# Front of a hybrid decoder step rewritten: token squares on two engines, first unit tile beside the gate tile, first head ahead of the branch product, recurrent turns at fixed tiles, padded rows

## The chip, the core and the metric

The kernel runs on one core of a Trainium2 chip. The core has five engines with their own instruction queues, which run each queue in order: TensorE (PE, with its weight loads as PEld), VectorE (DVE), ScalarE (ACT), GpSimd (POOL) and SyncE (SP), which here only issues DMAs. They meet at semaphores. TensorE writes to PSUM; the other data lies in SBUF. The metric is the device time of one execution in microseconds; 1193.46 us is the median of three runs of the kernel before (1191.86 to 1193.92).

## What is computed

One step of a hybrid decoder layer over 592 tokens: 16 meta tokens and 512 prompt tokens in one sequence, and 8 samples of 8 tokens with their own states. Width is 1024. Cut to what matters here:

```python
xn = rms_norm(x, norm1_g)
z  = xn @ w_in + b_in         # u | q | k | v | o | i-gate | f-gate | merge gate A | merge gate B
uc = causal_dwconv(u, lru_conv_buf, lru_conv_w, lru_conv_b)        # width 4
r, i = sigmoid(blockdiag(uc, w_r) + b_r), sigmoid(blockdiag(uc, w_i) + b_i)
a  = exp(-8 * r * softplus(-lambda))
h_t = a_t * h_{t-1} + sqrt(1 - a_t**2) * (i_t * uc_t)              # RG-LRU, scan over positions
hb = mlstm(q, k, v, i-gate, log_sigmoid(f-gate))                   # 4 heads, chunks, running max
merged = sigmoid(gA) * (h @ w_branch_a) + sigmoid(gB) * (hb @ w_branch_b)
x = x + merged @ w_out
x = x + ConvFFN(rms_norm(x, norm2_g))
```

Each prompt row starts from zero states, each sample from the states given; all new states are outputs.

## The kernel before

Everything is held with features on the 128 partitions and the 592 tokens along the row (T; two halves of 296 for PSUM). Products are made in split precision: a weight tile of 1024 x 128 arrives in `stage` (two slots) by a DMA on SP's queue (`load`, L429), ScalarE copies its high part to `whi` (`hi`, L744), GpSimd subtracts it to get the low part `wlo` (`lo`, L715), and TensorE multiplies high by high, high by low and low by high in 48 matmuls (`split_product`, L1675; `gemm`, L1686). Weight tiles and PSUM tiles are each numbered; `begin` (L1670) waits until the PSUM tile two places earlier is evicted, and `hi` for a weight tile waits until the tile two places earlier, which used the same slot, is finished. These numbers are constants (`B_U`, `T_U` and so on), and each engine's list is written out by hand in its own block.

The front of the layer, up to the first mLSTM score, runs in this order on TensorE: transposes of the token rows, with the tile of the two small gates (`gate_step`) between them; transposes of parameter rows; eight unit tiles (u); eight merge-gate tiles (A); eight branch tiles (h @ w_branch_a); eight tiles of the first head (k, v, q, o) with token-major copies of k and v; transposes of the gate rows. Before it, ScalarE squares the five token tiles one after the other and takes roots (L769), and VectorE scales by the reciprocals (L1122).

The recurrence works on one feature tile at a time, a turn: VectorE's convolution over prompt and samples apart (`conv`), TensorE's four gate matmuls into `bank`, ScalarE's two sigmoids, tanh and exponential, VectorE's products, ScalarE's root, VectorE's scan over time, ScalarE's high part and VectorE's low part of h. The unit and merge-gate tiles run in loops of pairs with one turn in each pair (`with_lru`, `u_pair`, `ga_pair`). One pair of buffers `ri` and `th` serves all turns. The gate weights of a turn (`lru_load`) are loaded by four DMAs between two weight tiles, after TensorE has finished the turn before:

```python
sp.wait_ge(w_lo, b - 1)
load(b, (b0 + j) % 2, w_in, ds(c0 + 256 * i + 128 * j, P))
if j == 0:
    sp.wait_ge(lru_ps, p)
    lru_load(p)
```

VectorE's chain for the mLSTM gates (`log1p_exp`, running maximum, running sum, `gate_rows`) stands behind the eight branch evictions. Its result goes through a DRAM buffer to SBUF (`spread_load`) for the head loop.

## Time and profile before

| | before |
|---|---|
| median of three runs | 1193.46 us |
| the profiled execution, its own time | 1192.03 us |
| its span, first to last instruction | 1190.1 us |
| mean granted clock of TensorE | 0.989 |
| TensorE busy | 1136.5 us |
| start of the first unit tile | 34.43 us |
| start of the first mLSTM score | 290.41 us |

TensorE is busy nearly all the time, so the profile is read by its idle and slowed stretches: what a wait of TensorE is put down to, and which engine's queue that engine's instruction stood in. "Busy" of an overlapped engine (VectorE's instructions that stand still behind GpSimd count as busy) says little alone.

### The profile page before, as it was taken

The numbers are of one execution on the slowest core, as the hardware profiler recorded it, in microseconds if no ns is written. First come the engines' busy times: TensorE is split into PE (matmuls) and PEld (weight loads), VectorE is DVE, ScalarE is ACT, GpSimd is POOL, SyncE is SP. The second block draws the span as 40 slices with busy tenths as digits, with TensorE's granted clock in tenths as the row PEclk, the third lists the DMA queues.
The fourth block names the chain that finished last, engine by engine and source line by source line (L and its number), as shares of the span: only waits on it lengthen the run. The fifth ranks groups of instructions, "written<-read, shape, count | busy, mean of one in ns | idle before, by whom it ended". The sixth has DMA issues, their size and how long they took to land.

```text
span 1190.1 us, 20521 instructions
## 1 busy us (share of the span) xinstructions
PE 1136.5 (95%) x8286; PEld 1106.4 (93%) x8286; DVE 652.3 (55%) x1056; ACT 403.4 (34%) x503; POOL 357.6 (30%) x163
## 2 busy tenths in 40 slices
PE   4997998999999999999998999999999999999996
PEld 4896998999999999989988999999999999999996
DVE  3689553273226328146264333999991069999302
ACT  5566891135323322323132333322221122222213
POOL 3132223433221313122212334433334334343420
PEclk9998999999999999999998999999999999999998
DMA  6122222226136235244244233322323222323312
GB/s 161 39 75 54 60 73 71 76 75 184 53 86 202 59 111 172 54 124 134 54 133 135 73 89 90 89 80 82 102 84 98 69 75 71 89 72 101 88 35 84
DMA packets 181030, 108.76 MB, mean 91 GB/s; under 512 B 8981, under 2 KB 177381, under 8 KB 180952
## 3 DMA queue, kind: packets, MB, share of 16 engines
q1 hardware_dynamic: 180952, 107.63, 31.4%
q8 instruction: 60, 0.98, 0.3%
q14 instruction: 18, 0.15, 0.0%
HBM read 95.19 MB, written 12.41 MB: 90 GB/s over the span
## 4 chain that ended last, share of the span: by engine, by line
PE 83%; issue 11%; DVE 3%; POOL 2%; ACT 1%; POOLq 0%; ACTq 0%; DVEq 0%
PE ring L1682 36%; PE ring L2072 21%; PE bank L2072 16%; POOL wlo L718 2%; PE bank L1895 2%; PE bank L1880 1%; PE bank L1944 1%; PE ring L1787 1%; PE bank L1864 1%; PE bank L1849 1%; PE bank L1922 1%; PE bank L1884 1%; PE bank L1872 1%; DVE y L1119 1%; DVE n_tmp L1446 0%
## 5 line engine op out<-in xcount | busy, mean ns | idle before, releaser
L718 POOL TENSOR_TENSOR wlo<-stage,whi 128x1024 fp32r<-128x1024 f32 x80 | 195.1, 2440 | 527.1 <-ACT whi L749 527.1
L1682 PE MATMUL ring<-xh,whi 128*128 128x296 f32 x1024 | 233.3, 309 | 15.6 <-POOL wlo L718 12.5
L1682 PE MATMUL ring<-xh,wlo 128*128 128x296 f32 x1024 | 224.7, 301 | 0.0
L1682 PE MATMUL ring<-xl,whi 128*128 128x296 f32 x1024 | 224.7, 301 | 0.0
L1682 PEld LDWEIGHTS ring<-xh,whi 128*128 128x128 f32 x1024 | 167.4, 191 | 28.2 <-issue 20.2
L1682 PEld LDWEIGHTS ring<-xl,whi 128*128 128x128 f32 x1024 | 168.5, 191 | 0.0
L1682 PEld LDWEIGHTS ring<-xh,wlo 128*128 128x128 f32 x1024 | 167.9, 190 | 0.0
L736 POOL TENSOR_TENSOR wlo<-stage,whi 128x1024 fp32r<-128x1024 f32 (+1 forms) x40 | 105.8, 2647 | 176.1 <-ACT whi L1032 176.1
L749 ACT ACTIVATE whi<-stage 128x1024 fp32r<-128x1024 f32 x81 | 85.2, 1052 | 47.9 <-PE ring L1682 35.7
L1032 ACT ACTIVATE whi<-stage 128x1024 fp32r<-128x1024 f32 (+1 forms) x40 | 45.9, 1151 | 94.4 <-PE ring L2072 59.2
L736 POOL TENSOR_TENSOR wlo_third<-stage,whi_third 128x1024 fp32r<-128x1024 f32 (+1 forms) x20 | 51.4, 2572 | 87.1 <-ACT whi_third L1032 87.1
L1119 DVE SCALAR_TENSOR_TENSOR conv<-up,cols,conv 128x608 f32<-128x608 f32 x88 | 74.9, 852 | 3.1
L2072 PE MATMUL ring<-xh,whi 128*128 128x296 f32 x256 | 56.0, 300 | 0.0
L1065 ACT ACTIVATE conv<-conv 128x608 f32<-128x608 f32 x22 | 15.7, 713 | 118.3 <-DVE conv L1119 118.3
L2072 PE MATMUL ring<-xh,wlo 128*128 128x296 f32 x256 | 55.7, 299 | 0.0
L2072 PE MATMUL ring<-xl,whi 128*128 128x296 f32 x256 | 55.6, 299 | 0.0
L1657 DVE TENSOR_TENSOR resid<-ring,resid 128x592 f32<-128x592 f32 x10 | 7.7, 774 | 86.6 <-PE ring L2072 86.6
L1433 DVE COPY hb<-bank 128x256 f32<-128x256 f32 (+1 forms) x20 | 8.0, 402 | 83.9 <-PE bank L1884 74.5
L1631 DVE TENSOR_TENSOR product<-conv 128x528 f32<-128x528 f32 x22 | 53.0, 2411 | 0.0
L1603 DVE COPY up<-cols 128x16 f32<-128x16 f32 x44 | 45.4, 1031 | 0.0
L2072 PE MATMUL bank<-xh,whi 128*128 128x296 f32 x192 | 42.0, 300 | 0.0
L2072 PE MATMUL bank<-xh,wlo 128*128 128x296 f32 x192 | 41.7, 299 | 0.0
(337 smaller groups left out, 2389.5 us busy)
## 6 DMA issues: line engine op xcount, KB each, us to landing
stage<-in_w_in SPq DMA_DIRECT2D x56, 512.0 KB, 3.8
stage<-in_w_up SPq DMA_DIRECT2D x44, 512.0 KB, 3.8
stage<-in_w_down SPq DMA_DIRECT2D x16, 704.0 KB, 4.6
c_sample<-in_state_mlstm_C SPq DMA_DIRECT2D x24, 256.0 KB, 3.5
out_s_mlstm_C<-c_sample SPq DMA_DIRECT2D x24, 256.0 KB, 2.2
stage<-in_w_branch_a SPq DMA_DIRECT2D x8, 512.0 KB, 4.1
stage<-in_w_branch_b SPq DMA_DIRECT2D x8, 512.0 KB, 4.2
stage<-in_w_out SPq DMA_DIRECT2D x8, 512.0 KB, 4.1
```

The lines of the kernel that those rows point to most:

```text
L718: pool.tensor_tensor(wlo[:, slot, 0:n], stage[:, slot, 0:n], whi[:, slot, 0:n].bitcast(F32), ALU.subtract).then_inc(w_lo, 1)
L736: pool.tensor_tensor(l_[:, 0:n], stage[:, b % 2, 0:n], w_[:, 0:n].bitcast(F32), ALU.subtract).then_inc(w_lo, 1)
L749: act.activation(whi[:, slot, 0:n], stage[:, slot, 0:n], ACT.Copy).then_inc(w_hi, 1)
L1032: act.activation(ffn_weight(i)[0][:, 0:n], stage[:, b % 2, 0:n], ACT.Copy).then_inc(w_hi, 1)
L1065: act.activation(cv[:, 1, 0:CV_N], cv[:, 1, 0:CV_N], ACT.Gelu_apprx_tanh).then_inc(gelu_done, 1)
L1119: return stt(out=out, in0=in0, scalar=scalar, in1=in1, op0=op0, op1=op1)
L1603: st(cpy(grouped(U[:, US0:UW_F - UG], UG)[:, :, 0:FW - 1], hist[:, :, ft:ft + UPT + 1:UPT]))
L1631: tt(pr[:, 0:TP], cv[:, 0, 0:TP], cv[:, 1, 0:TP], ALU.mult).then_inc(prod_done, 1)
L1682: last = pe.matmul(out(hf), w[:, slot, kk * P:kk * P + P], x[:, kk, HALF * hf:HALF * hf + HALF], start=kk == 0 and m == 0, stop=kk == kn - ...
L1787: last = pe.transpose(wide[t % 2][0:L, at + DH * (c - chunks[0]) + P * jj:][:, 0:P], src[:, jj, P * c:P * c + L], ident[:, :])
L1895: lz = pe.matmul(Z[:, 256 * ii:256 * ii + 256], kw[kappa % 2][0:L, P * ii:P * ii + P], vt[s][0:L, c, :], start=True, stop=True)
L2072: last = pe.matmul(z[:, hf, 0:HALF], w_[:, kk * P:kk * P + P], x_[:, kk, HALF * hf:HALF * hf + HALF], start=kk == 0 and m == 0, stop=kk == ...
```

## The change

Only the front is rewritten; from the first score on the work is the same. In its parts:

- Start: the eleven parameter loads of the first group are issued by ScalarE instead of SP. ScalarE squares token tiles 0, 2 and 4, VectorE squares 1 and 3. The gate tile's weight goes to a third pair of buffers (`whi_third`, `wlo_third`), its conversion stands behind the second feature tile, and the first unit tile is computed into `bank` step by step beside the gate tile.
- All recurrent gate weights are loaded once, into two buffers of eight tiles. The loops over pairs are written out. Turn p's matmuls stand ahead of tile `LRU_TURN[p]`, its exponential, root and split before the weights of tile `LRU_EXP[p]`, `LRU_ROOT[p]`, `LRU_SPLIT[p]`; `lru_i` and `lru_tanh` have two buffers.
- Padded rows: u and the convolution hold prompt and samples in one row of 616 columns, each sample with its three earlier columns ahead, so that a convolution is four instructions and the scan starts each sample in its padding. The u eviction is in three pieces, the splits in two.
- The first head's eight tiles come before the eight branch tiles. The gate chain on VectorE is cut in pieces between branch evictions, its first piece ahead of all of them. State transposes go to `bank` after the first branch tile.

The order of instructions at three places. In the rows, x2 is a count; a name without an arrow's right side is written from nothing. First TensorE at the end of the token transposes: the last gate steps and the parameter rows, before:

```order
L1682 MATMUL bank<-xl,whi 128x296 x2
L1682 MATMUL bank<-xh,wlo 128x296 x2
L1696 MATMUL ring<-ident,rows 128x108
L1696 MATMUL ring<-ident,rows 128x88
L1696 MATMUL ring<-ident,rows 128x44
L1696 MATMUL ring<-ident,rows 128x96 x2
L1696 MATMUL ring<-ident,rows 128x88 x8
L1682 MATMUL ring<-xh,whi 128x296 x2
```

and after, where `whi_third` is the gate tile's weight and `whi` that of the first unit tile:

```order
L1758 MATMUL bank<-xh,wlo 128x296 x2
L1772 MATMUL ring<-ident,rows 128x108
L1772 MATMUL ring<-ident,rows 128x88
L1772 MATMUL ring<-ident,rows 128x44
L1772 MATMUL ring<-ident,rows 128x96 x2
L1772 MATMUL ring<-ident,rows 128x88 x2
L1758 MATMUL bank<-xh,whi_third 128x296 x2
L1758 MATMUL bank<-xl,whi_third 128x296 x2
L1758 MATMUL bank<-xh,wlo_third 128x296 x2
L1758 MATMUL bank<-xh,whi 128x296 x2
L1758 MATMUL bank<-xl,whi 128x296 x2
L1758 MATMUL bank<-xh,wlo 128x296 x2
```

The unit tile's steps have moved from behind the parameter rows to between them. Second, ScalarE in the first head from the second v tile to the first q tile (a weight's high half is `whi`, the numbers behind names are buffers), before:

```order
L765 ACTIVATE k_tok_77<-ring 128x1024
L749 ACTIVATE whi<-stage 128x1024
L765 ACTIVATE v_feat<-ring,cols 128x592
L749 ACTIVATE whi<-stage 128x1024
L765 ACTIVATE q_71<-ring,misc 128x592
L765 ACTIVATE v_tok_79<-ring 128x1024
```

and after:

```order
L798 ACTIVATE v_feat<-ring,cols 128x592
L885 ACT_TABLE_LOAD
L885 ACTIVATE u<-lru_r,misc 128x616
L890 ACT_TABLE_LOAD
L890 ACTIVATE lru_tanh_81<-lru_tanh_81 128x616
L992 ACT_TABLE_LOAD
L992 ACTIVATE gate_scratch<-gate_scratch 4x592
L782 ACTIVATE whi<-stage 128x1024
L798 ACTIVATE q_61<-ring,misc 128x592
L798 ACTIVATE v_tok_69<-ring 128x1024
```

Turn 7's exponential, turn 6's root and the gate exponential have moved in between, and the conversion now waits for the tile that the eviction behind it reads. Third, VectorE around the last turn's low part (`hl`) and the branch evictions (`merged`), before:

```order
L1232 TENSOR_TENSOR hl<-uc,hh 128x592
L1268 TENSOR_TENSOR merged<-ring,merged 128x592 x2
L1274 TENSOR_REDUCE misc<-ident 80x8
L1276 MEMSET back 128x128
L1279 COPY back<-ident 32x8 x8
L1282 COPY misc<-misc 80x1
L1284 TENSOR_TENSOR misc<-misc 80x1 x2
```

and after:

```order
L1289 TENSOR_TENSOR cols<-uc,hh 128x64
L1292 CAST hl<-cols 128x64
L1203 TENSOR_SCALAR gate_scratch<-gate_scratch 4x592
L1204 RECIPROCAL gate_scratch<-gate_scratch 4x592
L1205 TENSOR_TENSOR gate_scratch<-gate_scratch 4x592
L1206 TENSOR_TENSOR gate_scratch<-gate_scratch 4x592
L1207 TENSOR_SCALAR gate_scratch<-gate_scratch 4x592
L1176 SCALAR_TENSOR_TENSOR gate_scratch<-gate_scratch 4x592 x8
L1211 TENSOR_SCALAR gate_scratch<-gate_scratch 4x592
L1306 TENSOR_SCALAR gate_scratch<-gate_scratch 4x592
L1307 TENSOR_TENSOR gate_scratch<-gate_scratch 4x592
L1370 TENSOR_TENSOR merged<-ring,merged 128x592
```

Before, the first two evictions follow the last low part at once (the rows behind them make constants), and the gates' logarithm stands behind all eight; after, it stands ahead of the first. The core of the diff:

```diff
+LRU_TURN = (3, 6, 9, 11, 13, 15, 17, 19)
+LRU_EXP = (4, 7, 10, 12, 14, 16, 18, 20)
+LRU_ROOT = (5, 8, 12, 14, 16, 18, 20, 21)
+LRU_SPLIT = (6, 9, 13, 15, 17, 19, 21, 22)
+U0 = LW - 1
+US = U0 + TP
+UGR = LW - 1 + LS
+UW = US + UGR * NB
+UN = UW - (LW - 1)
+UH = UN // 2
...
@@ sync
+            for g in range(1, 28):
+                main_load(g)
+            sp.wait_ge(lc_ready, 1)
+            sp.dma_start(o["p_lru_conv"][0, 0], conv_out[0:3, :]).then_inc(lru_out, 16)
+            sp.dma_start(o["s_lru_conv"][0].rearrange("b j c -> (b j) c"), conv_out[3:27, :]).then_inc(lru_out, 16)
+            sp.dma_start(o["p_lru_h"].rearrange("l b (f c) -> (l b f) c", c=P), h_out[0:8, :]).then_inc(lru_out, 16)
+            sp.dma_start(o["s_lru_h"].rearrange("l b (f c) -> (l b f) c", c=P), h_out[8:72, :]).then_inc(lru_out, 16)
+            for g in range(28, 31):
+                main_load(g)
...
+            spread_load(0)
+            main_load(31)
+            head_load(8)
+            head_load(9)
+            sp.wait_ge(lru_out, 64)
+            sp.wait_ge(tile_done, T_WA + 8)
+            spread_load(1)
...
@@ scalar
+            st(act.activation(misc[:, 207:208], eps, ACT.Sqrt))
+            for i in range(TT):
+                n = P if i < TT - 1 else LAST
+                if i % 2 == 0:
+                    act.wait_ge(x_in[i], 32 if i in (0, TT - 1) else 16)
+                    if i:
+                        st.wait()
+                    st(act.activation(sq_tok[0][0:n, :], x_tok[0:n, i], ACT.Square, accum_out=ss[0:n, i:i + 1]))
+                    st.wait()
+                else:
+                    act.wait_ge(x_sq, i // 2 + 1)
+                act.activation(rms[0:n, i:i + 1], ss[0:n, i:i + 1], ACT.Sqrt, scale=1.0 / D,
+                               bias=eps[0:n]).then_inc(rms_done, 1)
...
+            def lru_period(g):
+                for p in range(8):
+                    if LRU_EXP[p] == g:
+                        lru_decay(p)
+                for p in range(8):
+                    if LRU_ROOT[p] == g:
+                        lru_root(p)
+                for p in range(8):
+                    if LRU_TURN[p] == g:
+                        lru_sigmoids(p)
+                for p in range(8):
+                    if LRU_SPLIT[p] == g:
+                        lru_split(p)
+            def evict_u(g):
+                t = T_U + g
+                z = bank[:, 2:4] if g == 0 else ring[:, t % 2]
+                bias = cols[:, C_BIN + g:C_BIN + g + 1]
+                act.wait_ge(tile_done, t + 1)
+                st(act.activation(u[:, g, U0:U0 + HALF], z[:, 0, 0:HALF], ACT.Identity, bias=bias))
+                st(act.activation(u[:, g, U0 + HALF:US], z[:, 1, 0:TP - HALF], ACT.Identity, bias=bias))
+                act.wait_ge(tile_evicted, t)
+                act.activation(u[:, g, US:UW].rearrange("p (b l) -> p b l", l=UGR)[:, :, LW - 1:],
+                               z[:, 1, TP - HALF:HALF].rearrange("p (b l) -> p b l", l=LS), ACT.Identity, bias=bias
+                               ).then_inc(tile_evicted, 1)
+            def main_hi(g):
+                b = B_U + g + 2
+                hi(b, b % 2, D, main_tile(g) + 1, loads_of(b))
...
+            for g in range(31):
+                if g:
+                    lru_period(g)
+                if g == 20:
+                    act.wait_ge(gate_abs, 1)
+                    act.activation(gs[:, 2, :], gs[:, 2, :], ACT.Exp, scale=-1.0).then_inc(gate_exp, 1)
+                main_hi(g)
+                t = main_tile(g)
+                if g < 8:
+                    evict_u(g)
+                elif g < 16:
+                    f = g - 8
+                    evict(t, h2(merged[:, f]), rt(t % 2), ACT.Sigmoid, bias=cols[:, C_BGA + f:C_BGA + f + 1])
+                elif g < 24:
+                    project(g - 16)
+                    if g == 18:
+                        k_tokens(0)
+                    elif g == 20:
+                        v_tokens(0)
+                elif g == 24:
+                    act.wait_ge(lc_done, 1)
+                    st(act.activation(conv_out[:, :], bank2(0)[0:27, :], ACT.Copy))
+                    act.activation(h_out[:, :], bank2(1)[0:72, 0:P], ACT.Copy).then_inc(lc_ready, 1)
+            spread(0)
...
@@ vector
+            for i in (1, 3):
+                dve.wait_ge(x_in[i], 16)
+                dve.wait_ge(const_done, 1)
+                if i > 1:
+                    dve.wait_ge(x_sq, 1)
+                stt(out=sq_tok[1][:, :], in0=x_tok[:, i], scalar=1.0, in1=x_tok[:, i], op0=ALU.mult, op1=ALU.mult,
+                    accum_out=ss[:, i:i + 1]).then_inc(x_sq, 1)
+                for i_ in (i - 1, i) if i == 1 else (2, 3, 4):
+                    n = P if i_ < TT - 1 else LAST
+                    dve.wait_ge(rms_done, i_ + 1)
+                    st.link(dve.reciprocal(rms[0:n, i_:i_ + 1], rms[0:n, i_:i_ + 1]))
+                    ts(x_tok[0:n, i_], x_tok[0:n, i_], rms[0:n, i_:i_ + 1], None, ALU.mult).then_inc(x_scaled, 1)
...
+            def conv(f):
+                dve.wait_ge(tile_evicted, T_U + 1 + f)
+                if f == 0:
+                    st.wait()
+                w = [cols[:, C_CW + 8 * m + f:C_CW + 8 * m + f + 1] for m in range(LW)]
+                st(cpy(ulast[:, f, :].rearrange("p (n l) -> p n l", l=LW - 1),
+                       u[:, f, US - UGR:UW].rearrange("p (n l) -> p n l", l=UGR)[:, :, LS:]))
+                st.link(ts(uc[:, f], u[:, f, 0:UN], w[0], cols[:, C_CB + f:C_CB + f + 1], ALU.mult, ALU.add))
+                for m in range(1, LW - 1):
+                    st.link(mul_add(uc[:, f], u[:, f, m:m + UN], w[m], uc[:, f]))
+                mul_add(uc[:, f], u[:, f, LW - 1:UW], w[LW - 1], uc[:, f]).then_inc(conv_done, 1)
...
+            def lru_scan(p):
+                i_, x, a_ = ig_[p % 2], uc[:, p], u[:, p, 0:UN]
+                dve.wait_ge(lru_sq, p + 1)
+                st.link(tt(i_[:, :], i_[:, :], th[p % 2][:, :], ALU.mult))
+                st(cpy(before(i_), cols[:, C_H0:C_H0 + 64].rearrange("p (b f) -> p b f", f=8)[:, :, p]))
+                st(dve.memset(before(a_), 0.0))
+                st.wait()
+                dve.tensor_tensor_scan(out=x, data0=a_, data1=i_[:, :], initial=0.0, op0=ALU.mult, op1=ALU.add
+                                       ).then_inc(lru_h, 1)
+                dve.wait_ge(lru_h, p + 1)
+                st(cpy(hlast[:, :, p], x[:, TP - 1:UN:UGR]))
...
+            lru_rates()
+            conv(0)
+            conv(1)
+            for g in range(3, 23):
+                for p in range(8):
+                    if LRU_EXP[p] == g:
+                        lru_square(p)
+                if g - 1 < 8:
+                    conv(g - 1)
+                for p in range(8):
+                    if LRU_ROOT[p] == g:
+                        lru_scan(p)
+                for p in range(8):
+                    if LRU_SPLIT[p] == g:
+                        lru_lo(p)
+                if g == 19:
+                    gates_abs()
+            gates_log()
+            evict_wa(0)
+            gates_max()
+            evict_wa(1)
+            gates_sum()
+            evict_wa(2)
+            gates_rows()
+            evict_wa(3)
+            gates_inter()
+            evict_wa(4)
+            sample_constants()
+            evict_wa(5)
+            evict_wa(6)
...
@@ tensor
+            for f in range(8):
+                begin(T_XN + f)
+                token_transposes(wide[(T_XN + f) % 2], f, x_tok).then_inc(tile_done, 1)
+                if f >= 3:
+                    gate_step(f - 3)
+                if f >= 4:
+                    first_step(f - 4)
+            pe.wait_ge(rows_in[1], 16 * 7)
+            row_transposes(T_COLS2, *COL_GROUPS[1])
+            gate_step(5)
+            first_step(4)
+            row_transposes(T_COLS2 + 1, *COL_GROUPS[2])
+            gate_step(6)
+            gate_step(7).then_inc(tile_done, 1)
+            for kk in (5, 6):
+                first_step(kk)
+            first_step(7).then_inc(tile_done, 1)
...
+            for g in range(1, 16):
+                if g in LRU_TURN:
+                    lru_gates(LRU_TURN.index(g))
+                gemm(B_U + g, T_U + g, (B_U + g) % 2, (T_U + g) % 2, KT, xh, xl)
...
+            for n in range(8):
+                if 16 + n in LRU_TURN:
+                    lru_gates(LRU_TURN.index(16 + n))
+                fill(0, n)
+                if n == 2:
+                    k_tokens(0)
+                elif n == 4:
+                    v_tokens(0)
+            for f in range(8):
+                t = T_WA + f
+                gemm(B_WA + f, t, (B_WA + f) % 2, t % 2, KT, hh, hl, None if f else lambda kk: pe.wait_ge(lru_lo_, kk + 1))
+                if f == 0:
+                    pe.wait_ge(lru_sig, 8)
+                    for m in range(8):
+                        pe.transpose(bank2(0)[0:27, P * m:P * m + P], ulast[:, m, :], ident[:, :])
+                    pe.transpose(bank2(1)[0:72, 0:P], stage[:, 0, D + 224:D + 224 + 72], ident[:, :]).then_inc(lc_done, 1)
...
```

## Rows read from the trace of the kernel before

**Rows 1.** The page, busy us, share of the span, instructions.

```profile
PE 1136.5 (95%) x8286; PEld 1106.4 (93%) x8286; DVE 652.3 (55%) x1056; ACT 403.4 (34%) x503; POOL 357.6 (30%) x163
```

**Rows 2.** TensorE's waits, 41 to 291 us: total, times, longest.

```profile
PE ring L1682 <- POOL wlo L718: 8.2, 4, 2.8
PE ring L1682 <- DVE hl L1232: 4.8, 1, 4.8
PE bank L1736 <- ACT u L824: 3.1, 2, 2.0
PE ring L1682 <- ACT conv_out L765: 0.9, 1, 0.9
PE bank L1736 <- DVE uc L1119: 0.7, 1, 0.7
PE ring L1682 <- ACT v_tok L765: 0.6, 1, 0.6
```

**Rows 3.** Timeline of ScalarE: start, us, instruction [idle before and what ended it].

```profile
57.81 1.06 ACT L749 ACTIVATE whi<-stage 128x1024 fp32r<-128x1024 f32 x1 [2.86 <-DMA stage<-in_w_in]
```

**Rows 4.** SP's own waits, 0 to 291 us.

```profile
SPq L502 <- PE bank L1736: 92.1, 7, 28.9
```

**Rows 5.** Windows: busy us (instructions) of PE, PEld, DVE, ACT, POOL; PEclk; DMA.

```profile
41.00:112.00 71.00, 63.41 (x424) 59.77 (x423) 58.71 (x104) 43.05 (x49) 19.10 (x7) 1.00 0.24 64
111.00:122.00 11.00, 8.15 (x31) 6.97 (x30) 10.48 (x24) 7.12 (x7) 5.18 (x2) 0.53 0.21 54
183.00:187.00 4.00, 3.92 (x17) 3.92 (x18) 0.80 (x2) 1.06 (x1) 1.04 (x1) 0.57 0.14 40
41.00:291.00 250.00, 231.69 (x1594) 223.68 (x1593) 150.08 (x241) 133.69 (x152) 77.16 (x31) 0.97 0.29 79
```

**Rows 6.** Timeline of TensorE, starts of the pieces that the sum uses.

```profile
15.73 1.25 PE L1707 MATMUL ring<-ident,x_tok 128*128 128x128 f32 x5 [0.89 <-DVE x_tok L1126]
...
34.43 0.51 PE L1682 MATMUL ring<-xh,whi 128*128 128x296 f32 x2 [0.50 <-ACT cols L785]
...
148.78 2.16 PE L1736 MATMUL bank<-uc,lru_gate_w 128*128 x8
150.56 0.65 PE L1682 MATMUL ring<-xh,whi 128*128 128x296 f32 x2
...
207.49 0.44 PE L1682 MATMUL ring<-hh,whi 128*128 128x296 f32 x2
...
233.71 0.44 PE L1682 MATMUL ring<-xh,whi 128*128 128x296 f32 x2
...
267.79 1.04 PE L1787 MATMUL ring<-ident,v_feat 128*128 128x128 f32 x8
...
290.41 0.61 PE L1849 MATMUL bank<-q,k 128*128 128x128 f32 x4
```

**Rows 7.** ScalarE's groups, 100 to 182 us: count, busy us, mean ns.

```profile
L765 ACT ACT_TABLE_LOAD x8 | 10.3, 1283 | 1.3 <-PE ring L1682 1.1
...
L765 ACT ACTIVATE merged<-ring,cols 128x592 f32 x8 | 6.0, 755 | 0.1
...
L830 ACT ACTIVATE lru_tanh<-lru_tanh 128x592 f32<-128x592 f32 x5 | 3.5, 698 | 0.1
```

**Rows 8.** Timeline of GpSimd and VectorE.

```profile
152.48 2.40 POOL L718 TENSOR_TENSOR wlo<-stage,whi 128x1024 fp32r<-128x1024 f32 x1 [2.65 <-ACT whi L749]
...
152.59 2.33 DVE L1228 COPY stage<-uc  x1 [0.18 <-DVE uc L1225]
...
243.33 0.46 DVE L1139 TENSOR_SCALAR gate_scratch<-gate_scratch 4x592 f32<-4x592 f32 x1 [5.18 <-ACT gate_scratch L950]
...
261.46 0.76 DVE L1298 TENSOR_TENSOR gate_scratch<-gate_scratch 4x592 f32<-4x592 f32 x1
```

**Rows 9.** The page's groups: the convolution of the later stage.

```profile
L1119 DVE SCALAR_TENSOR_TENSOR conv<-up,cols,conv 128x608 f32<-128x608 f32 x88 | 74.9, 852 | 3.1
```

**Rows 10.** Timeline of SP at the start.

```profile
4.31 0.83 SPq L464 DMA_DIRECT2D rows<-in_norm_g  x2
```

565 lines of the change are left out of this document (228 added, 337 removed).

## The prediction

> **What bounds the kernel now.** The first view is the page: TensorE is busy for 1136.5 of 1190.1 us [rows 1], so only its idle or slowed time can go. The second is TensorE's waits between 41 and 291 us, from the second unit tile to the first mLSTM score [rows 2]: six causes, 18.3 us. Four waits (8.2) are for GpSimd's low half of a weight tile, three (3.8) for the recurrence's other engines, one (4.8) for the last recurrent tile before the branch product. What lies behind the first is seen at 57.81 [rows 3]: ScalarE, free, made the high half 2.86 us later because the load came late; SP's own waits show why, seven of 92.1 us in total for a recurrent turn on TensorE [rows 4], with the weight loads queued behind them. The third view, windows, shows two stretches at a granted clock of 0.53 and 0.57 [rows 5], so mostly at the lower of the two levels, 1.2 GHz, and each follows such waits. From 41 to 291 us VectorE is busy for 150.1 us and ScalarE for 133.7 of 250, so neither is full over the whole, but in the unit stretch, 41 to 112, VectorE has 58.7 of 71.
>
> **The floor of the new stretch.** A tile of 48 products: four of them start at 207.49 and end at 233.71, so 6.555 us each [rows 6]. A recurrent turn: from 148.78 to 150.56, 1.78 us; with 616 columns for 592, 1.85 (estimate by width). Transposes: eight at 267.79 took 1.04, 0.13 each; states, k, v with its tail and gate rows are 34, so 4.4. After the change TensorE does, from the end of the first unit tile to the first score, 31 tiles (203.2), 8 turns (14.8) and these 4.4: 222.4 us. Before, the first unit tile began at 34.43, so ended at 41.0, and the first score began at 290.41: 249.4. The floor is 27.0 lower. Of that, 18.3 are the waits and 5.5 the low clock (busy 8.15 at 0.53 and 3.92 at 0.57: 8.15 x 0.47 + 3.92 x 0.43); padding takes back 0.6; 3.8 I can't place (loop edges and refilling after ten waits are likeliest).
>
> **Part 1, recurrent turns at fixed tiles; all gate weights loaded once.** SP's seven waits on TensorE go, and with them eight times four loads between weight loads. A turn's matmuls now stand two or more tiles after the convolution they read, its exponential, root and split at later numbered tiles. A weight tile must be ready 6.56 us after the tile two ahead ends; high half 1.06 and low half 2.40 take 3.46 [rows 3, 8], so ScalarE may be 3.1 late without cost. ScalarE's fullest merge-gate period has exponential, root and sigmoid with a table load each: 3 x 1.28 + 0.8 (exponential, like the other passes) + 0.70 + 0.76 + 1.06 = 7.2 [rows 3, 7], and its neighbour 5; two such periods with a turn last 15.0. It keeps up. The cover is VectorE: while GpSimd subtracts, VectorE's instructions on SBUF stand still, as the two rows at 152.5 show (a copy of nine columns took 2.33) [rows 8]. Per period that is 2.2. A padded convolution is 0.16 + 0.64 + 3 x 0.85 = 3.4 (from the 608-column row [rows 9], small parts estimated by width); the rest of a turn, three passes of 0.8, a product, a scan of twice its time and the split, about 6.1. Tiles 3 to 8 hold six convolutions, two squares, two scans, one split and six stops: 44.9 us for 43.0 of TensorE. It ends 1.9 behind, inside the 3.1. Over tiles 3 to 22 it is 113 for 146. I take 0 here; the rival below is that the rows are too kind.
>
> **Part 2, the first head ahead of the branch product.** The wait of 4.8 for the last turn goes: its last split is due at tile 22 and read at tile 24. What comes instead: ScalarE now converts weights before it evicts. At tile 20 it has, after tile 19's end, 1.06 + 0.76 (weights, v) and then exponential, root and the gate exponential, a table each: 3 x 1.28 + 0.8 + 0.70 + 0.7 = 6.0. It is 1.3 late when tile 20 ends, evicts q 3.1 after that, and TensorE, whose v transposes end after 1.04, waits 2.1 for the tail's buffer and 0.5 more for v: **2.6 us new**. Queued behind on ScalarE are the root of turn 7 and split 6; the chain goes on to VectorE: split 7 is ready 2.8 after tile 21, its low part 4.8 after, then the gates' logarithm. In the trace that ran from 243.33 to 262.2, 18.9 with two stops [rows 8]; with three, 21.1. The first branch eviction, queued behind it, ends 26.7 after tile 21; TensorE needs it after four tiles and the state transposes, 27.5. Margin 0.8: 0 to 1.3 if the chain is a tenth longer. SP holds the last branch weight behind the gate rows; it lands about when needed, with 2.7 to spare. Likewise the decay rates (some twenty instructions of 0.2, estimated) end about 4 after the first unit tile, the first padded convolution with one or two stops 10 to 12, and turn 0 needs it at 13.1: 0 to 1.2. For these two I take 1.0 together.
>
> **The clock.** From 41 to 112 us TensorE was idle for 7.6 of 71 with a granted clock of 1.00; the fall at 111 came beside the longest waits of two kinds, 2.8 and 2.0 [rows 2, 5], and cost 8.15 x 0.47 = 3.8. The new 2.1 and 0.5 lie between; I take half, 1.9, with 0 and 3.8 as bounds.
>
> **Part 3, the start.** ScalarE now issues eleven parameter loads; two took SP 0.83 [rows 10], so 4.6; then one table load instead of two. From 0.7, when SP could start: 5.3, table and root 6.8, square and root 8.4. VectorE squares tiles 1 and 3 (about 1.25 each, from 0.85 for 608; bounds 1.1 and 1.5) between scalings of 1.0 each, and the second square waits for its tile to land: the last tile is scaled at 14.8, or about 15.7 as before (transposes from 15.73 [rows 6]) if that tile is late. So the squares gain 0 to 0.9. Then two groups of five transposes at 1.25, a conversion of 0.8, the high half behind the second feature tile (1.06) and the low half (2.4): first gate product at 21.9. From it to the end of the first unit tile TensorE has 16 steps of 0.82 (an eighth of a tile), four groups of five transposes (2.6) and 13 of parameters (1.7): 17.4, and 1 to 2 more while the array starts slowly (five transposes took 1.25 at 15.73, eight took 1.04 at 267.79). End at 40.6, against 41.0: 0.4 gained, bounds 1.5 either way.
> The Trainium skill (Trainium Kernel Development and Optimization, Key Constraints) says that loads issued from several engines share the same 16 DMA engines and only issue time is saved. By that rule moving the loads makes x land no sooner and the term stays 0.4; if a second queue did bring x sooner, the term would be near its bound of 1.9. No row of before shows which.
>
> **Sum.** -27.0 + 2.6 + 1.0 + 1.9 - 0.4 = -21.9. The profiled execution took 1192.03 (span 1190.1): 1170.1. The median of the runs is 1193.46, 1.4 above it: **1171.5**. Nothing after the first score changes its work; its sample-state loads now wait for the last branch tile but are needed some 35 us on.
>
> **Rivals.** (1) *VectorE falls behind in the unit stretch.* For: 58.7 of 71 already, and each subtraction stops it. If its instructions are 20% dearer than the rows, tiles 3 to 8 cost 6.3 more: 8.2 behind with 3.1 allowed, so 5.1 of weight waits; the gate chain is 2 past its margin, the first convolution 1; sum 8, 1179.5. Against: dependent rows follow each other within 0.05. (2) *The gate chain ends last.* It is one serial list behind split 7; each us past 0.8 costs one, and past 3 also the last branch weight. At 6 longer: 5 to 6, 1177. Against: the same instructions had 18.9. (3) *The waits do not go* (another late load or buffer takes each place): half of 27.0 stays, 1185. (4) *Slower than before:* VectorE with its stops bounds every period from tile 3 to 22. It decides only where its 113 us become more than 146 + 22 = 168, half as much again; at 1.6 times 113, 181 us, the stretch is 35 longer than its floor and the time 1204. For it speaks only that the stops are counted from one place.
>
> **How the numbers follow.** Forecast with its own range 1166 to 1176: 0.68. Rival 1: 0.13, rival 2: 0.07, rival 3: 0.08, rival 4: 0.04. The low end has no clock loss and no small waits (2.9 less), the start's bound (1.5) and half of the wait at tile 20 (1.3): 1166. The high end takes in rivals 1 and 2: 1182. About 0.2% (2.4 us) is what a measurement can tell from no change. Faster 0.93 (all but rival 4 and a part of 3), same 0.03, slower 0.04.
>
> **What would show it.** TensorE's waits for the low halves, for u and for hl are gone from 41 us on, a wait of about 2 at the tail transposes of the first head is there, the first score is near 268.5, and the first unit tile ends between 39 and 42. It is wrong if VectorE is busy without pause from 60 to 110, if the branch tiles wait for evictions, or if the half clock returns.

## The result, and the profile after

The changed kernel takes 1171.38 us, the median of four runs (1170.74 to 1173.68); the kernel before took 1192.83 beside it (also the median of four). The ratio is 0.9823, with a 95% interval of 0.9806 to 0.9841. Predicted were 1171.5, 1166 to 1182. The profiled execution took 1171.94, with a span of 1169.8, 20.3 below the span before.

The page's first line, and TensorE's waits from the second unit tile to the first score (total, times, longest, us), which answer to [rows 1, 2]:

```profile
PE 1133.6 (97%) x8286; PEld 1107.0 (95%) x8286; DVE 652.3 (56%) x1012; ACT 391.0 (33%) x513; POOL 363.7 (31%) x164
```

```profile
PE ring L1848 <- ACT q L798: 2.2, 1, 2.2
PE ring L1758 <- ACT v_tok L798: 0.5, 1, 0.5
```

Five of the six causes of before are gone. The wait for `v_tok` stands where it stood (0.5 for 0.6), and the one for `q` is new. The same stretch in windows (us, busy us and instructions of PE, PEld, DVE, ACT, POOL, then the granted clock), to be read against [rows 5]:

```profile
192.80:196.10 3.30, 2.95 (x12) 2.98 (x13) 0.49 (x1) 3.27 (x7) 0.95 (x1) 0.50 0.30 80
111.00:122.00 11.00, 11.00 (x76) 10.45 (x75) 0.96 (x2) 6.26 (x8) 2.38 (x2) 1.00 0.34 90
41.00:112.00 71.00, 71.00 (x500) 69.34 (x500) 59.28 (x83) 41.51 (x62) 25.80 (x10) 1.00 0.29 77
```

TensorE is busy for 71.0 of 71 us in the unit stretch (63.4 before), and up to the first score one stretch at 1.2 GHz is left, 3.3 us behind the two waits. VectorE's busy time there hardly moved (59.3 for 58.7), but the last of its eight convolutions was over at 98.9 us, where before it ended at 118.2.

TensorE's pieces by their starts (start, us, instruction, and in brackets the idle time before and what ended it), as in [rows 6]:

```profile
15.17 2.23 PE L1783 MATMUL ring<-ident,x_tok 128*128 128x128 f32 x10 [1.99 <-DVE x_tok L1190]
...
40.13 0.43 PE L1758 MATMUL ring<-xh,whi 128*128 128x296 f32 x2
...
142.35 1.20 PE L1823 MATMUL bank<-uc,lru_w_r 128*128 128x308 f32 x4
...
144.19 0.67 PE L1758 MATMUL ring<-xh,whi 128*128 128x296 f32 x2
145.24 0.44 PE L1758 MATMUL ring<-xh,whi 128*128 128x296 f32 x2
...
157.55 1.20 PE L1823 MATMUL bank<-uc,lru_w_r 128*128 128x308 f32 x4
...
188.81 1.03 PE L1848 MATMUL ring<-ident,v_feat 128*128 128x128 f32 x8
192.01 0.41 PE L1848 MATMUL ring<-ident,k 128*80 128x128 f32 x2 [2.17 <-ACT q L798]
...
193.15 0.83 PE L1758 MATMUL ring<-xh,whi 128*128 128x296 f32 x2 [0.51 <-ACT v_tok L798]
...
268.39 0.38 PE L1922 MATMUL bank<-q,k 128*128 128x128 f32 x2
```

The first unit tile ends at about 40.1 (the next begins at 40.13) and the first score starts at 268.39: 228.3 us where 249.4 were.

### The profile page after: what moved, and what is told of

Its sections match the earlier page's. It is cut to its first block, busy times and chain, and to the rows that moved or that the text cites. A ratio compares the mean times of both kernels' runs of the same rounds, so it can differ in the third digit from the quotient of the medians.

```text
span 1169.8 us, 19900 instructions
## 1 busy us (share of the span) xinstructions
PE 1133.6 (97%) x8286; PEld 1107.0 (95%) x8286; DVE 652.3 (56%) x1012; ACT 391.0 (33%) x513; POOL 363.7 (31%) x164
## 3 DMA queue, kind: packets, MB, share of 16 engines
q8 instruction: 65, 1.06, 0.4%
## 4 chain that ended last, share of the span: by engine, by line
PE 92%; DVE 3%; issue 2%; POOL 1%; ACT 1%; POOLq 0%; DVEq 0%; ACTq 0%
PE ring L1758 42%; PE ring L2145 21%; PE bank L2145 16%; PE bank L1968 2%; PE bank L1823 1%; PE bank L1953 1%; PE bank L1758 1%; PE bank L2017 1%; PE bank L1937 1%; PE bank L1922 1%; PE bank L1995 1%; PE ring L1848 1%; PE bank L1957 1%; PE bank L1945 1%; DVE y L1176 1%
## 5 line engine op out<-in xcount | busy, mean ns | idle before, releaser
L1758 PE MATMUL ring<-xh,whi 128*128 128x296 f32 x1008 | 229.9, 310 | 6.7 <-POOL wlo L745 4.3
L1758 PE MATMUL ring<-xh,wlo 128*128 128x296 f32 x1008 | 221.2, 301 | 0.0
L1758 PE MATMUL ring<-xl,whi 128*128 128x296 f32 x1008 | 221.0, 301 | 0.0
L1758 PEld LDWEIGHTS ring<-xh,whi 128*128 128x128 f32 x1008 | 164.9, 191 | 17.4 <-issue 9.3
L1758 PEld LDWEIGHTS ring<-xl,whi 128*128 128x128 f32 x1008 | 165.8, 191 | 0.0
L1758 PEld LDWEIGHTS ring<-xh,wlo 128*128 128x128 f32 x1008 | 165.3, 191 | 0.0
L2145 PE MATMUL ring<-xh,whi 128*128 128x296 f32 x256 | 56.0, 300 | 0.0
L2145 PE MATMUL ring<-xh,wlo 128*128 128x296 f32 x256 | 55.7, 299 | 0.0
L2145 PE MATMUL ring<-xl,whi 128*128 128x296 f32 x256 | 55.7, 299 | 0.0
```

The source lines that it names most:

```text
L1758: last = pe.matmul(out(hf), w[:, kk * P:kk * P + P], x[:, kk, HALF * hf:HALF * hf + HALF], start=kk == 0 and m == 0, stop=kk == kn - 1 and ...
L2145: last = pe.matmul(z[:, hf, 0:HALF], w_[:, kk * P:kk * P + P], x_[:, kk, HALF * hf:HALF * hf + HALF], start=kk == 0 and m == 0, stop=kk == ...
```

## The experiments

Each kernel is the changed one with the edit shown. Its measure is the stretch from the second unit tile to the first score, 228.3 us in the changed kernel, because what lies before and behind it varies from profile to profile: the stretch began between 39.32 and 41.52 us, and 899.3 to 903.2 us followed the first score where the work behind it was the same. Two of the kernels ran several times (both edits of the next part together, and the branch product first); of the others there is one run each, read by its profile.

### ScalarE's order at the end of the first head

The forecast's new wait was put down to ScalarE's list at tile 20. In the trace after (ScalarE: start, us, instruction):

```profile
184.23 1.28 ACT L885 ACT_TABLE_LOAD   x1
185.52 0.81 ACT L885 ACTIVATE u<-lru_r,misc 128x616 f32<-128x616 f32 x1
186.35 1.28 ACT L890 ACT_TABLE_LOAD   x1
187.65 0.72 ACT L890 ACTIVATE lru_tanh<-lru_tanh 128x616 f32<-128x616 f32 x1
188.38 1.28 ACT L992 ACT_TABLE_LOAD   x1
189.68 0.69 ACT L992 ACTIVATE gate_scratch<-gate_scratch 4x592 f32<-4x592 f32 x1
190.28 1.04 ACT L782 ACTIVATE whi<-stage 128x1024 fp32r<-128x1024 f32 x1
191.23 0.73 ACT L798 ACTIVATE q<-ring,misc 128x592 f32<-128x592 f32 x1
191.99 1.02 ACT L798 ACTIVATE v_tok<-ring 128x1024 f32<-128x1024 f32 x1
```

Three table loads and three passes end at 190.28, 1.4 after tile 20 (whose transposes follow at 188.81); the conversion comes next and q is free at 192.0. Two edits, first apart and then together:

```diff
 # in lru_period, between exponentials and roots (VectorE makes its input at 15, not 19)
+                if g == 16:
+                    act.wait_ge(gate_abs, 1)
+                    act.activation(gs[:, 2, :], gs[:, 2, :], ACT.Exp, scale=-1.0).then_inc(gate_exp, 1)
...
-                if g == 20:
-                    act.wait_ge(gate_abs, 1)
-                    act.activation(gs[:, 2, :], gs[:, 2, :], ACT.Exp, scale=-1.0).then_inc(gate_exp, 1)
```

```diff
-                main_hi(g)
+                if g not in (18, 20):
+                    main_hi(g)
...
                     elif g == 20:
                         v_tokens(0)
+                    if g in (18, 20):
+                        main_hi(g)
```

The gate exponential earlier:

> Only the gate exponential is moved to period 16; weights are still converted before evictions. My account: ScalarE is free 0.5 before tile 20 ends instead of 1.3 after, so q is evicted 1.8 after its tile: wait for q 0.8 to 1.0, for v 0.4 to 0.5. First score 266.9 if the half clock stays, 265.2 if a wait of about 1 does not bring it. Rival (the exponential is late for VectorE or keeps another conversion back in period 16): a new wait near 160 to 167 us, first score 268 or more.

Measured: waits of 0.98 for q and 0.51 for v, first score at 265.32, stretch 225.7. The granted clock stayed at 1.00:

```profile
189.30:195.00 5.70, 4.22 (x30) 3.99 (x31) 5.55 (x7) 3.76 (x8) 2.88 (x1) 1.00 0.21 61
```

Evictions ahead of the conversion:

> Only the order at tiles 18 and 20 is changed: evictions ahead of the conversion; the gate exponential stays at tile 20. My account: ScalarE still comes 1.3 late, then evicts q at once: wait for q 1.1 to 1.3, for v 0.3 to 0.5, first score 267.2, or 265.5 without the half clock. Rival (the conversion, now 2.5 later, is late for tile 22): a low-half wait near 200 us.

Measured: waits of 1.22 and 0.51, no half clock behind them, stretch 225.9; the first score came at 266.63, 1.1 above the 265.5 expected, and 0.6 of that is a later start of the second unit tile (40.70). No low half was late.

Both:

> Changed: the gate exponential stands with turn 5's exponential (period 16) and needs no table of its own, and at tiles 18 and 20 ScalarE evicts before it converts the next weights. My account (ScalarE's queue at tile 20 makes the new wait, and the half clock follows from the wait): TensorE's wait for q at the last rows of the first head falls from 2.17 to under 0.3, the wait for v stays near 0.5 (its eviction, 1.0, is longer than the 0.63 of transposes beside it), the half clock of 3.4 us at 193 us does not come; the first score is at 268.4 - 2.2 - 1.7 = 264.5 and the time near 1167.3. Rival (the wait is only moved, since the weights of tiles 20 and 22 are converted later): low-half waits of about 2 at tiles 20 or 22 and a time of 1171. Rival on the clock (the half clock has nothing to do with this wait): first score at 266.2 and a time near 1169.

Measured: one wait is left, and ScalarE, now free before tile 20 ends, evicts q at once:

```profile
PE ring L1760 <- ACT v_tok L798: 0.6, 1, 0.6
```

```profile
188.25 0.76 ACT L798 ACTIVATE q<-ring,misc 128x592 f32<-128x592 f32 x1 [0.70 <-PE ring L1760]
189.12 1.02 ACT L798 ACTIVATE v_tok<-ring 128x1024 f32<-128x1024 f32 x1
```

The first score starts at 264.19, the stretch is 224.9. The kernel takes 1168.41 (1167.22 to 1169.14, five runs), ratio to the kernel before 0.9797 (0.9776 to 0.9818): 3 us below the changed kernel, whose runs lie all above, though in another comparison. So the wait, its cause and the half clock behind it are what the account said; the time came 1.1 above the expected 1167.3.

### What had made the low halves late before

The prediction followed the first of these waits to SP: the load came late because it stood behind SP's wait for a recurrent turn [rows 3, 4]. First that is undone alone:

```diff
             for g in range(1, 28):
+                if g in LRU_TURN[1:]:
+                    p = LRU_TURN.index(g)
+                    sp.wait_ge(lru_ps, p)
+                    lru_load(p)
                 main_load(g)
```

> The recurrent gate weights are loaded again turn by turn on SP's queue, ahead of the weights of the turn's own tile and behind a wait for the turn before, as in the kernel before; the turns stay at their fixed tiles and have a buffer each. Theory A (SP's waits for TensorE made the low-half waits, as the prediction said of the row at 57.81): loads come late again and 4 to 8 us of low-half waits return before 190 us. Theory B (the spread of a turn's steps removed them, and SP's wait only showed it): the turn before stands two tiles ahead of the tile whose load waits for it, the load lands within those two tiles, and nothing returns: first score 268.4 to 269.

SP now waits for TensorE again (its own waits, total, times, longest):

```profile
SPq L523 <- PE bank L1831: 64.7, 7, 11.5
```

64.7 us of waits, with 92.1 before [rows 4], and they cost nothing: the stretch is 228.5, TensorE's waits are the two of the changed kernel. The longest is 11.5, though, where before it was 28.9, and the load that came late at 57.81 [rows 3] stood behind that one. So the kernel does not put back the first low-half wait of before (2.13, ending at 61.42). Second, the turns are drawn together as before:

```diff
-LRU_TURN = (3, 6, 9, 11, 13, 15, 17, 19)
-LRU_EXP = (4, 7, 10, 12, 14, 16, 18, 20)
-LRU_ROOT = (5, 8, 12, 14, 16, 18, 20, 21)
-LRU_SPLIT = (6, 9, 13, 15, 17, 19, 21, 22)
+LRU_TURN = (3, 5, 7, 9, 11, 13, 15, 17)
+LRU_EXP = (3, 5, 7, 9, 11, 13, 15, 17)
+LRU_ROOT = (4, 6, 8, 10, 12, 14, 16, 18)
+LRU_SPLIT = (5, 7, 9, 11, 13, 15, 17, 19)
```

with the exponential behind the sigmoids on ScalarE, and scan, convolution, low part and square in that order on VectorE.

> The gate weights stay loaded once, but a turn's steps are drawn together as in the kernel before: turns ahead of tiles 3, 5, 7 and so on to 17, the exponential with the sigmoids, the root one tile later, the split two tiles later, so that ScalarE stands waiting for VectorE's scan inside a pair of tiles. Theory B (it was the nearness of a turn's steps that kept ScalarE from the weights): low-half waits and waits for the banks or u come back between 55 and 190 us, 4 to 12 us in all, and the first score is at 273 to 282. Theory A (SP's queue made them): no wait comes back, first score 268 to 269.

Measured: none of the old waits came back, and the stretch is 227.0 (first score 267.62). What is left stands in the first head, and without the half clock:

```profile
PE ring L1756 <- ACT v_feat L798: 1.1, 1, 1.1
PE ring L1846 <- ACT q L798: 1.0, 1, 1.0
PE ring L1756 <- ACT v_tok L798: 0.5, 1, 0.5
```

As undone here, neither theory had held, so a third was formed: VectorE set the pace of the unit tiles. It is read from the starts of one instruction of a turn. In the trace before:

```profile
81.72 0.78 DVE L1216 TENSOR_TENSOR ri<-ri,lru_tanh 128x592 f32<-128x592 f32 x1
...
101.11 0.78 DVE L1216 TENSOR_TENSOR ri<-ri,lru_tanh 128x592 f32<-128x592 f32 x1
```

19.4 us for a pair of tiles with a turn, which take TensorE 15.2 (142.35 to 157.55 above). In the window between the two VectorE is busy for 17.56 us, and its gaps are of 0.2, behind its own results; it waited for no other engine. Its busy time counts two short instructions, at 92.56 and 96.72, of 2.34 and 2.22 us beside GpSimd's subtractions:

```profile
81.72:101.11 19.39, 16.58 (x113) 15.53 (x113) 17.56 (x31) 11.29 (x13) 5.20 (x2) 1.00 0.32 86
```

ScalarE meanwhile stood for VectorE's scan (its waits, 41 to 140 us):

```profile
ACT hh L835 <- DVE uc L1225: 22.0, 4, 8.0
```

Behind three of these four waits (6.86, 8.00 and 5.62) it made the high halves whose low halves TensorE then waited for: 1.69, 2.85 and 1.48, ending at 94.98, 116.16 and 135.59, 6.0 of the 8.2 us. In the changed kernel the same product:

```profile
76.48 2.98 DVE L1272 TENSOR_TENSOR lru_i<-lru_i,lru_tanh 128x616 f32<-128x616 f32 x1
...
98.78 2.99 DVE L1272 TENSOR_TENSOR lru_i<-lru_i,lru_tanh 128x616 f32<-128x616 f32 x1
```

22.3 for three tiles with a turn, for 21.8 of TensorE's time. VectorE is as full here (21.76 of 22.30 in that window), but level with TensorE, and the last convolution is over at 98.8; behind it there is room (0.96 busy in the 11 us from 111, above). Three kernels test it. Both edits above together:

> Both undone: the turn's steps drawn together and the gate weights loaded turn by turn on SP's queue behind a wait for the turn before. If the two are each enough to hide the other's fault (theory AB), 4 to 12 us of low-half waits come back before 175 us and the first score lies at 272 to 280. Theory C (VectorE set the pace of the unit tiles before, about 20 us for a pair of tiles that takes TensorE 15, and padded rows with less in each pair took that away; ScalarE and SP only stood behind it): nothing beyond the other run of tight turns, first score 267.6 to 268.6.

Measured: stretch 227.0, first score 268.04: nothing beyond the tight turns alone. With tight turns alone the product starts at 66.69, 84.35 and 101.84, so VectorE takes 17.5 to 17.7 for a pair, more than TensorE, and over these pairs no low half is late. Then the tight turns with the work on VectorE that separate rows had cost:

```diff
                 if g - 1 < 8:
                     conv(g - 1)
+                    st.link(mul_add(spare, spare, 1.0, spare))
+                    st.link(mul_add(spare, spare, 1.0, spare))
```

> Turns drawn together, gate weights loaded once, and two more passes of 616 columns behind each of the six convolutions from the third on: 1.6 us a tile, a little more than what separate rows of prompt and samples cost (4.45 for a convolution against 3.4, and 0.3 in the scan). Theory C: a pair of unit tiles takes VectorE 6.8 + 3.2 + 6.2 + two stops of 2.2 = 20.6 for TensorE's 15.1, so over three pairs it falls 16 behind with some 7 allowed: 6 to 10 us of waits for low halves, u or the banks between 70 and 130 and, as before, a half clock behind them: first score 274 to 281. Theory AB: nothing comes back while the loads are made once, first score 267.6 to 268.6.

The low halves are late again, though the gate weights are loaded once:

```profile
PE ring L1759 <- POOL wlo L745: 5.9, 4, 2.3
PE ring L1759 <- ACT v_feat L798: 2.5, 1, 2.5
```

```profile
67.50 0.80 DVE L1270 TENSOR_TENSOR lru_i<-lru_i,lru_tanh 128x616 f32<-128x616 f32 x1 [0.79 <-ACT lru_tanh L890]
...
88.63 0.80 DVE L1270 TENSOR_TENSOR lru_i<-lru_i,lru_tanh 128x616 f32<-128x616 f32 x1 [0.79 <-ACT lru_tanh L890]
```

VectorE takes 21.1 for a pair (20.6 expected); first score 277.16, stretch 237.5, 10.5 more than with tight turns alone. The four waits end between 103.24 and 139.80, and their 5.9 us match the 6.0 of before. ScalarE stands for VectorE again, though mostly one step earlier, ahead of its root (17.4 us) and less for the scan (6.3). Last, the same passes with the turns spread:

> The same two more passes behind six convolutions, with the turns at the tiles of the changed kernel (a turn each third tile there instead of each second). Theory C: a pair of unit tiles takes VectorE 6.8 + 3.2 + 4.1 + 4.4 = 18.5 for 15.1, over three pairs 10 behind with some 7 allowed: 0 to 4 us of waits, first score 268.4 to 273. If the spread is worth nothing, the same waits as with the turns drawn together, first score 274 or more.

Measured: one wait of 1.98 for a low half at 116.04, first score 270.71, stretch 230.7. The weight of that tile was converted at 112.53, behind ScalarE's wait for the scan:

```profile
111.83 0.64 ACT L895 ACTIVATE hh<-uc 128x528 fp32r<-128x528 f32 x1 [8.84 <-DVE uc L1277]
```

So three of the four low-half waits of before were VectorE's: its pair was 4 longer than TensorE's, ScalarE stood for its scans, and weights were converted late behind that. Padded rows (by the time they save VectorE) and a turn for every third unit tile both shorten it, and either alone leaves little of the waits. The first wait of before, 2.13, lies in its trace behind SP's late load, and no kernel here puts that load back. The second buffers of `lru_i` and `lru_tanh` were kept in all of them, so what they do is not shown.

### How much more VectorE could take

One and three extra passes of 616 columns in each of VectorE's steps 3 to 22 (the line of the diff above, in the loop over g):

> One more pass of 616 columns on VectorE (0.8 us, on its own scratch) in each of its steps 3 to 22: 16 us, a seventh more work there. By the prediction's count VectorE ends tiles 3 to 8 at 44.9 + 4.8 = 49.7 for 43.0, 6.7 behind with 3.1 allowed: 3.6 us of waits, first score near 272. By the idle time of the trace after (12.3 us of VectorE between 40 and 112, behind waits for the exponentials): nothing, first score 268.4.

Measured: stretch 228.4, nothing; the first score stands at 269.93 only because the second unit tile began at 41.52.

> Three more passes of 616 columns on VectorE in each of its steps 3 to 22: 48 us, more with the stops behind GpSimd. By the prediction's count (113 + 48 = 161 for 146, decisive from 168) the unit stretch is 13 us late and the rest hides most: first score 278 to 285. By the idle time of the trace after, 14.4 us and 3 of stops into 12.3 plus what is allowed late: first score 268.4 to 273. If the slower side of the prediction (VectorE bounds every period) is near, the first score is above 290.

Measured: first score 283.24, stretch 242.2, 13.9 more:

```profile
PE ring L1761 <- POOL wlo L745: 5.8, 2, 5.7
PE ring L1851 <- ACT q L798: 4.7, 1, 4.7
PE ring L1761 <- ACT v_feat L798: 1.6, 1, 1.6
```

and a granted clock of 0.50 from within each of the two long waits on (119.9 to 126.7 and 205.2 to 212.0 us). The first score lies in the range that went with the prediction's count; with one more pass it was the reckoning by idle time that held. Up to the last convolution 4.9 more us of VectorE (six passes) cost nothing, 9.8 cost 2.0 and 14.7 cost 5.8 of low-half waits: about 8 us were free (an estimate, 9.8 less 2.0 and 14.7 less 5.8).

### The first head and the branch product

```diff
-            for n in range(8):
-                if 16 + n in LRU_TURN:
-                    lru_gates(LRU_TURN.index(16 + n))
-                fill(0, n)
...
             for f in range(8):
                 t = T_WA + f
...
+            for n in range(8):
+                fill(0, n)
...
+LRU_TURN = (3, 5, 7, 9, 10, 12, 13, 15)
+LRU_EXP = (4, 6, 8, 10, 11, 13, 14, 15)
+LRU_ROOT = (5, 7, 9, 11, 12, 14, 15, 16)
+LRU_SPLIT = (6, 8, 10, 12, 13, 15, 16, 16)
```

VectorE's gate chain stands behind the eight branch evictions again, its exponential at tile 18.

> The branch product is put back ahead of the first head, the gate chain back behind the branch evictions, the gate exponential to a branch tile; the turns are placed as early as their steps allow (3, 5, 7, 9, 10, 12, 13, 15), all else as changed. My account (the order saves the wait for the last turn's low part, 4.8, and costs 2.6 at tile 20): the low part of turn 7 is late by 3 to 5 us at the first branch product, the wait for q falls to about 0.5, that for v stays 0.5; fuller periods ahead of tile 16 cost 0 to 3 more and a half clock up to 1.7: first score 269 to 275, time 1172 to 1178. Rival (the order is worth nothing, a turn that ends at tile 16 hides its last steps as well): first score 266 to 267, 2 below the changed kernel's, time 1169.

Measured: 1186.35 us (1185.07 to 1187.09), ratio 0.9931 (0.9904 to 0.9957), first score 279.77, beyond the range of both theories.

```profile
PE ring L1753 <- DVE hl L1291: 9.1, 2, 5.7
```

Two turns' low parts are late, 5.7 and 3.3, and TensorE is at 1.2 GHz (granted clock 0.50) from 162 to 175 us. The stretch is 11.6 longer with this table of turns. The kernel before, in the same order, waited 4.8 for the last low part [rows 2], so part of the 11.6 is the table's: another might lose less, none was tried, and what the order alone is worth stays open.

### The start, and the gate chain

Three edits that lie apart in one kernel: squares all on ScalarE, the first unit tile's steps all behind the gate tile, and 13 copies of 4 x 592 in VectorE's gate chain ahead of the first branch eviction.

```diff
-                if i % 2 == 0:
-                    act.wait_ge(x_in[i], 32 if i in (0, TT - 1) else 16)
+                act.wait_ge(x_in[i], 32 if i in (0, TT - 1) else 16)
...
-                if f >= 4:
-                    first_step(f - 4)
...
                 log1p_exp(yy, s3, s4, s5)
+                for _ in range(13):
+                    st.link(cpy(s4, s3))
```

> Three undone or lengthened places that lie apart. Start: all five squares on ScalarE again: token transposes begin at 15.2 to 16.0 (15.17 with two engines), since the last tiles land late in both. First unit tile behind the gate tile instead of beside it: TensorE has the same work, so its end stays at 40.3 plus the later start if no wait for evictions comes in, and is 1 to 2 later if one does. Gate chain on VectorE longer by 13 copies of 0.46, 6.2 with what lies between: by the trace the first branch eviction has 1.8 to spare, so the third branch tile waits 4.0 to 5 (up to 6.5 if one more low half stops the chain); by the prediction's margin of 0.8 it waits 5.4. First score 272.5 to 276 beside the shift of the start.

The gate chain behaved as written, only dearer, since two low halves stopped the copies (10.5 instead of 6.2). One of these stops had hit another instruction of the chain, so the chain from its first instruction to the end of the eviction is 8.4 longer (29.1 for 20.7):

```profile
223.69 10.50 DVE L1298 COPY gate_scratch<-gate_scratch 4x592 f32<-4x592 f32 x13
...
235.51 0.77 DVE L1363 TENSOR_TENSOR merged<-ring,merged 128x592 f32<-128x592 f32 x1
```

```profile
PE ring L1751 <- DVE merged L1363: 6.6, 1, 6.6
```

Branch tile 2 stood ready at 229.8 and waited 6.6, which is the 8.4 less the 1.8 to spare. The granted clock fell to 0.50 within the wait, which no sum had priced: the stretch is 9.7 longer, and the first score, 279.25, lies above the expected 272.5 to 276 even without the 1.15 by which the second unit tile began later.

The start is not settled. Transposes began at 15.46 and the second unit tile at 41.28. But in the kernels with an unchanged start these lay between 14.70 and 15.57, and between 39.32 and 41.52. TensorE's first products go at little more than half their later pace (in the changed kernel pairs of matmuls start 0.50 apart at 22.29 and 22.79, and 0.27 apart at 25.68 and 25.95), although the granted clock reads 1.00 there, and that slow stretch ended anywhere from 24.2 to 28.0 us. Whatever squares on two engines and the unit tile beside the gate tile bring is below that spread.

## Why the prediction came out right

| us, profile against profile | predicted | measured |
|---|---|---|
| floor of the stretch | 222.4 | 224.1 |
| new waits at tile 20 | 2.6 | 2.7 (2.17 + 0.51) |
| first convolution and gate chain | 1.0 | 0 |
| half clock | 1.9 | 1.5 (2.95 busy at 0.50) |
| the stretch | 227.9 | 228.3, so -21.1 |
| start | -0.4 | -0.9 |
| behind the first score | 0 | +1.7 |
| sum | -21.9 | -20.3 |

The floor measured is the stretch without its waits and half clock. The forecast one was 1.7 too low, and the size that was off is the turn. Its matmuls take 1.84, 142.35 to 144.19, as estimated; but the first step of the tile behind it lasts 1.05 (144.19 to 145.24) where steps take 0.82. A turn costs about 2.06, eight of them 1.7 more than counted. The same step took 1.03 to 1.04 before, behind turns without a wait, which explains part of the 3.8 us of before that could not be placed.

The wait at tile 20 was right in place, size and cause: 1.4 late where 1.3 was worked out, 2.17 and 0.51 where 2.1 and 0.5 were. Only the 0.51 is not new: it is the 0.6 for `v_tok` of [rows 2], taken out with the old waits and put back. The half clock's 1.9 was the middle between none and the 3.8 of before; it came, but held for 2.95 us of work where the one at 111 us had held for 8.15. The gate chain ended in time: on VectorE it started at 205.88, and the first branch eviction stood behind its last product.

```profile
205.88 0.45 DVE L1203 TENSOR_SCALAR gate_scratch<-gate_scratch 4x592 f32<-4x592 f32 x1
...
224.98 0.76 DVE L1307 TENSOR_TENSOR gate_scratch<-gate_scratch 4x592 f32<-4x592 f32 x1
225.78 0.78 DVE L1370 TENSOR_TENSOR merged<-ring,merged 128x592 f32<-128x592 f32 x1
```

The eviction was over at 226.6 and branch tile 2 began at 228.37: 1.8 to spare, 0.8 predicted. Rival 2's rule, each us past the margin costs one, held for the wait in the run with 13 copies (8.4 longer, 1.8 to spare, 6.6 waited), but not for the time, since a half clock came on top.

That the median, 1171.38, stands 0.1 from the 1171.5 forecast is luck. The profiled execution came 1.8 above its forecast (1171.94 for 1170.1; the misses in the table, of both signs, leave 1.6 in the span), and the median lies 0.6 below the profiled execution where 1.4 above it was taken.

Of the prediction's own signs of being wrong, one came about: the half clock returned, which its sum had priced. VectorE was busy for 40.2 of the 50 us from 60 to 110, so not without pause, but it waited for no engine from 66.3 to 103.7.

Two things were wrong in the reasons. **The cause of the old waits:** the prediction named SP's loads behind a turn [rows 3, 4]; that row was one case in four (2.13 of the 8.2 us), and loading turn by turn cost nothing where it was tried. The cause of the other three was VectorE's pace, which its busy share over the unit stretch (58.7 of 71, before and after alike) doesn't show. The start-to-start time of one instruction does. The forecast did not suffer, since the floor takes all waits away whoever made them. **VectorE's room:** the count of 44.9 for 43.0 left 1.2 us, so that rival 1 (20% dearer, 6.3 more) would cost 5.1; measured, some 8 us were free up to the last convolution. Rival 4 stays where it was: three passes more, 48 us, moved the first score to 283.24, short of the 290.41 of before.

What was taken as zero behind the first score came out at +1.7. The clock goes with it. In the same 40 us of work, from 321.6 us behind the first score on, the changed kernel had a granted clock of 0.87 and the kernel before 0.91:

```profile
590.00:630.00 40.00, 33.81 (x213) 32.94 (x212) 22.64 (x28) 12.12 (x21) 4.72 (x2) 0.87 0.46 140
```

```profile
612.00:652.00 40.00, 33.82 (x227) 32.91 (x226) 23.63 (x30) 13.36 (x21) 5.40 (x3) 0.91 0.46 140
```

The changed kernel has two stretches at 0.50 there, 6.8 us from 599 and 3.4 us from 619, the kernel before one, 6.3 us from 637. The kernel with the early exponential, the same from the first score on as the changed one, also had 0.91 (its window begins 3 us later in the work):

```profile
590.00:630.00 40.00, 33.80 (x231) 33.27 (x231) 21.42 (x27) 10.42 (x17) 7.11 (x3) 0.91 0.38 117
```

Of the kernels above some show the one and some the other, so nothing ties the 1.7 to the change.

The eleven parameter loads that ScalarE now issues brought the token rows no sooner (three prompt loads, last figure the median us to landing, after):

```profile
x_tok<-in_x_prompt SPq DMA_DIRECT2D x3, 512.0 KB, 7.0
```

It was 6.9 before. SP issues the token rows first in both kernels, from 0.7 to 4.3 us, ahead of the parameters, so moving these could not bring the rows' issue forward; the prediction's alternative, x landing sooner, had left that out. By the Trainium skill (Trainium Kernel Development and Optimization, Key Constraints) queues share the DMA engines and only issue time is saved; 7.0 against 6.9 fits that, but with the rows' issue unchanged no run here tests it.

## What to carry to other kernels

Where several engines wait for each other in a loop, take one instruction of each engine and read its start-to-start time: the engine whose own work fills that time sets the pace, however many other waits the profile names. Then ask how long it has to fall behind: 17.5 to 17.7 for TensorE's 15.2 cost no low-half wait here, 19.4 and 21.1 did. A floor made of the bound engine's pieces, plus the waits that the new order makes, forecast this rewritten stretch well (227.9, measured 228.3), although three of the four old low-half waits were explained wrongly. And convert or evict in the order in which TensorE needs the results: two edits on ScalarE's list were worth another 3 us.

## What the runs showed of the hardware

- Waits of 2.17 and 0.51 close together brought a granted clock of 0.50 each time, five of five (at 193 to 196 us in the changed kernel, and between 194 and 200 us in the runs with loads per turn, one extra pass, spread passes and 13 copies); 0.98 and 0.51, or 1.22 and 0.51, left it at 1.00.
- The length of a single wait does not tell whether the clock falls. Behind 1.97 (before, ending at 110.3 us) and 2.27 (tight turns with more on VectorE, at 103.2) it fell to 0.50; behind 1.98 (spread passes, at 116.0), 2.13 (before, at 61.4) and 2.45 (in the same run as the 2.27, at 186.9) it stayed at 1.00.
- A table load on ScalarE costs its 1.28 us and no more: the pass behind it starts 0.02 later (188.38 + 1.28, 189.68). The Trainium skill (ScalarE: Activation LUTs, What ACT_TABLE_LOAD costs) adds a drain of about 1.38 us to each switch; no row here shows that, and the measurement decides: with it tile 20's list would have ended 4.1 us later (an estimate, three times 1.38).
- Behind a turn's eight matmuls (128x308, from `uc`) the next product's first step took 1.04 to 1.06 for 0.82, in every turn of the changed kernel.
